# A pair of projection groups interleaved at the start, and the products with values in F32R parts

## What is computed

```python
xn = rmsnorm(h, norm_w[l], NORM_EPS)
proj = xn @ w_in[l]
o_ret = retention(rq, rk, rv).astype(h.dtype)        # (q k^T * decay) v, per head
o_ret = rmsnorm(o_ret, None, NORM_EPS).reshape(b, s, RET_WIDTH) * jax.nn.silu(rz)
o_diff = diff_attention(dq, dk, dv, lam)             # (softmax1 - lam * softmax2) v, per head
o_diff = rmsnorm(o_diff, subln_w[l], SUBLN_EPS) * (1.0 - lam_init) * jax.nn.silu(dz)
mixed = sigmoid(g_ret) * (o_ret @ w_ret_up) + sigmoid(g_diff) * (o_diff @ w_diff_up)
out = rmsnorm(h + mixed @ w_out, final_norm_w, NORM_EPS)
```

## Time and profile before

| | us |
|---|---|
| median of 3 runs (1103.31 to 1104.45) | 1103.32 |
| the profiled execution | 1103.43 |
| its span, from the first to the last instruction | 1101.6 |
| TensorE busy | 1088.8 |
| VectorE busy | 652.3 |
| ScalarE busy | 511.4 |

### The profile page before, as it was taken

How to read it: one execution, slowest core, us unless ns; L and a number is a source line. 1 busy time by engine, 2 the same in 40 slices (tenths; PEclk the granted TensorE clock), 3 DMA queues, 4 the chain that set the end, 5 groups by cost and what they waited for, 6 DMA issues and landing times.

```text
span 1101.6 us, 12909 instructions
## 1 busy us (share of the span) xinstructions
PE 1088.8 (99%) x4822; PEld 903.9 (82%) x4822; DVE 652.3 (59%) x785; ACT 511.4 (46%) x652; POOL 47.1 (4%) x64
## 2 busy tenths in 40 slices
PE   8999999999999999999999999999999999999997
PEld 6888888888888888888888888888888888888885
DVE  6665456475455554566656766576656665676554
ACT  6544444434445443334544464445444554444443
POOL 0100000000000000000010001000100010000111
PEclk9999999999999999999999999999999999999999
DMA  9876666667666655667566766766677666666862
GB/s 337 268 243 197 192 189 201 197 203 207 185 171 197 212 199 194 192 181 224 182 197 208 208 192 196 218 201 202 188 212 214 196 210 191 209 212 208 310 221 102
DMA packets 141030, 227.69 MB, mean 207 GB/s; under 512 B 14372, under 2 KB 40232, under 8 KB 140200
## 3 DMA queue, kind: packets, MB, share of 16 engines
q1 hardware_dynamic: 140408, 223.72, 66.1%
q10 hardware_dynamic: 560, 3.15, 0.7%
HBM read 210.58 MB, written 2.10 MB: 193 GB/s over the span
## 4 chain that ended last, share of the span: by engine, by line
PE 98%; DMA 1%; issue 1%; DVE 0%; SPq 0%; ACT 0%; ACTq 0%; POOLq 0%; POOL 0%; DVEq 0%
PE bank L1029 32%; PE bank L1031 31%; PE bank L1030 31%; PE bank L1036 1%; PE bank L1038 1%; PE bank L1037 1%; PE bank L1105 1%; DMA raw<-w_in_dram 1%; PE bank L1109 0%; PE bank L1060 0%; PE bank L1061 0%; DVE w_lo L706 0%; ACT w_hi L508 0%; ACT mixed L693 0%; DVE gate L958 0%
## 5 line engine op out<-in xcount | busy, mean ns | idle before, releaser
L706 DVE TENSOR_TENSOR w_lo<-raw,w_hi 128x1024 fp32r<-128x1024 f32 x383 | 474.2, 1243 | 421.3 <-ACT w_hi L508 420.3
L508 ACT ACTIVATE w_hi<-raw 128x1024 fp32r<-128x1024 f32 x383 | 405.7, 1060 | 549.6 <-PE bank L1031 518.1
L1029 PE MATMUL bank<-w_hi,xt_hi 128*128 128x512 f32 x1280 | 502.0, 392 | 2.8 <-DVE w_lo L706 2.8
L1031 PE MATMUL bank<-w_hi,xt_lo 128*128 128x512 f32 x1280 | 498.8, 390 | 0.0
L1030 PE MATMUL bank<-w_lo,xt_hi 128*128 128x512 f32 x1280 | 498.8, 390 | 0.0
L1029 PEld LDWEIGHTS bank<-w_hi,xt_hi 128*128 128x128 f32 x1280 | 240.6, 188 | 53.2 <-issue 3.5
L1031 PEld LDWEIGHTS bank<-w_hi,xt_lo 128*128 128x128 f32 x1280 | 240.7, 188 | 50.5
L1030 PEld LDWEIGHTS bank<-w_lo,xt_hi 128*128 128x128 f32 x1280 | 240.8, 188 | 49.5
L1029 PE MATMUL bank<-w_hi,ot_hi 128*128 128x512 f32 x256 | 99.6, 389 | 0.0
L1030 PE MATMUL bank<-w_lo,ot_hi 128*128 128x512 f32 x256 | 99.6, 389 | 0.0
L1031 PE MATMUL bank<-w_hi,ot_lo 128*128 128x512 f32 x256 | 99.6, 389 | 0.0
(11 more groups left out here) (99 smaller groups left out, 360.1 us busy)
## 6 DMA issues: line engine op xcount, KB each, us to landing
raw<-w_in_dram SPq DMA_DIRECT2D x287, 512.0 KB, 4.2
raw<-w_ret_up_dram SPq DMA_DIRECT2D x32, 512.0 KB, 4.2
raw<-w_diff_up_dram SPq DMA_DIRECT2D x32, 512.0 KB, 4.3
raw<-w_out_dram SPq DMA_DIRECT2D x32, 512.0 KB, 4.5
rot<-squares_t SPq DMA_DIRECT2D x96, 64.0 KB, 2.4
normed<-squares_t SPq DMA_DIRECT2D x48, 64.0 KB, 2.2
gate<-x_dram SPq DMA_DIRECT2D x2, 1024.0 KB, 9.0
kT<-squares_t SPq DMA_DIRECT2D x32, 64.0 KB, 2.2
```

What stands on the lines that cost most here:

```text
L508: act.activation(w_hi[:, s, :, :], raw[:, s, :, :], ACT.Copy).then_inc(hi_ready, 1)
L706: dve.tensor_tensor(w_lo[:, s, :, :], raw[:, s, :, :], w_hi[:, s, :, :].bitcast(F32), ALU.subtract) \
L1029: pe.matmul(bank[bk][:, :], hi, w_hi[:, s, kk, :], start=k == 0, stop=False)
L1031: return pe.matmul(bank[bk][:, :], lo, w_hi[:, s, kk, :], start=False, stop=k == KT - 1)
```

## The change

The first sixteen units, of the groups RQ and RK, are taken in a new order: first k-tiles 0 to 7 in pairs (RQ unit 0, RK unit 0, RQ unit 1, ...), then the rest of RQ, then the rest of RK. A pair of x tiles is thus needed at positions 0, 2, 4, 6 and 8 to 11. The second position is loaded and split in halves, as the first already was. The loads of x pairs, of the rows of x, of the rope tables and of decay move in SP's order; `square_x` moves from s = 6, 7 to 9, 10, and in the first iteration the rotation of Q from s = 10, 11 to 12, 13. `decay_sb` now lies in `gate`, where the rows of x were, and SP waits for their squares ahead of its load.

The products with values become three F32R passes each. ScalarE writes `v_hi` and the rounded part of the score maps (`read_keys_hi`, into the last k-tiles of `ot_hi`), VectorE the rests (`read_v_lo`, `read_keys_lo`), and the banks of the values are freed by VectorE's part. In attention the map is formed in `probs`, with one more step in its chain of waits, and VectorE's turning of it reads and writes contiguous runs.

```diff
 FIRST = UNITS - AHEAD
+ROTATE_Q = (12, 10)
...
+def pair_order():
+
+    for u in range(UNITS // 2):
+        for g in range(2):
+            yield g, u
+    for g in range(2):
+        for u in range(UNITS // 2, UNITS):
+            yield g, u
+
+
+PAIR = tuple(pair_order())
+X_PAIR_AT = {PAIR.index((0, j)): j for j in range(UNITS)}
+
+
+def unit_at(n):
+
+    return PAIR[n] if n < 2 * UNITS else (n // UNITS, n % UNITS)
 
 
...
-        decay_sb = sb("decay_sb", [P, HEADS, TOKENS])
...
-        v_sb = sb("v_sb", [P, BLOCKS, 2 * COLS])
+        v_hi = sb("v_hi", [P, BLOCKS, 2 * COLS], F32R)
+        v_lo = sb("v_lo", [P, BLOCKS, 2 * COLS], F32R)
...
+        decay_sb = gate[:, :, :].rearrange("p b n -> p (b n)")[:, 0:HEADS * TOKENS].rearrange("p (h t) -> p h t", h=HEADS)
...
-            return v_sb[:, a, COLS:COLS + 3 * P]
+            return probs[:, a * 6 * P:a * 6 * P + 3 * P]
...
-                s = u % RING
+                s = n % RING
...
+                elif n == 1:
+                    sp.dma_start(raw[:, s, 0, :], w[:, 0, col:col + COLS]).then_inc(half_landed[1], 16)
                     sp.dma_start(raw[:, s, 1:KU, :], w[:, 1:KU, col:col + COLS]).then_inc(raw_landed[s], 16)
...
-                        if s in (10, 11):
-                            turn_qk(qT, s - 10, ret_turns(it, 0))
+                        if s in (ROTATE_Q[it], ROTATE_Q[it] + 1):
+                            turn_qk(qT, s - ROTATE_Q[it], ret_turns(it, 0))
...
-                    if n in (1, 2, 3):
-                        load_x_t(sp, n, 1)
-                    if n in (4, 5):
-                        load_x_t(sp, 2 * n - 4, 2)
+                    if n in (2, 4, 6):
+                        load_x_t(sp, n // 2, 1)
+                    if n in (7, 9):
+                        load_x_t(sp, n - 3, 2)
...
-                    if n in (7, 8):
-                        b = n - 7
+                    if n in (10, 11):
+                        b = n - 10
                         sp.dma_start(gate[:, b, :], x[b * P:(b + 1) * P, :]).then_inc(x_landed, 16)
-                    if n == 9:
+                    if n == 12:
...
-                    if n == 14:
-                        sp.dma_start(decay_sb[:], decay).then_inc(decay_landed, 16)
+                    if n == 18:
+                        sp.wait_ge(x_squared, BLOCKS)
+                        sp.dma_start(decay_sb, decay).then_inc(decay_landed, 16)
...
-                    act.activation(v_sb[:, b, half * COLS:(half + 1) * COLS], bank[banks + b][:, :], ACT.Copy,
+                    act.activation(v_hi[:, b, half * COLS:(half + 1) * COLS], bank[banks + b][:, :], ACT.Copy,
                                    scale=x_rstd[:, b:b + 1]) \
-                       .then_inc(drained[banks + b], 1)
+                       .then_inc(v_hi_ready, 1)
+
+            def read_keys_hi(a, src, dst):
+                act.activation(dst, src, ACT.Copy).then_inc(keys_hi_ready, 1)
 
...
+                    if n0 + (s + AHEAD) in X_PAIR_AT:
+                        xt_hi_pair(X_PAIR_AT[n0 + (s + AHEAD)])
                     split_hi(n0 + (s + AHEAD), (s + AHEAD) % UNITS)
-                    if it == 0 and s in (6, 7):
-                        square_x(s - 6)
+                    if it == 0 and s in (9, 10):
+                        square_x(s - 9)
...
+                    if s in (36, 37):
+                        for m in range(2):
+                            act.wait_ge(drained[6 + m], ret_uses(it, 1) + 1)
+                        read_keys_hi(s - 36, scores_t(s - 36), keys_hi(s - 36))
+                    if s in (46, 47):
+                        act.wait_ge(filled[6 + s - 46], ret_uses(it, 2) + 1)
+                        read_keys_hi(s - 46, scores_t(s - 44), keys_hi(s - 46))
                     if s == 40:
...
+                    if s == 31:
+                        for a in range(2):
+                            act.wait_ge(turned[a], TURN * (diff_turns(it, 2) + 1))
+                            read_keys_hi(a, attn_strips(a), key_rows(keys_hi(a)))
...
+                elif event:
+                    dve.wait_ge(squares_ready[1], event)
...
+            def read_v_lo(count, banks, half):
+
+                for b in range(BLOCKS):
+                    cols = slice(half * COLS, (half + 1) * COLS)
+                    dve.wait_ge(v_hi_ready, count + (b + 1))
+                    dve.scalar_tensor_tensor(out=v_lo[:, b, cols], in0=bank[banks + b][:, :], scalar=x_rstd[:, b:b + 1],
+                                             in1=v_hi[:, b, cols].bitcast(F32), op0=ALU.mult, op1=ALU.subtract) \
+                       .then_inc(drained[banks + b], 1)
+
+            def read_keys_lo(count, src, hi, dst):
+
+                dve.wait_ge(keys_hi_ready, count + 1)
+                dve.tensor_tensor(dst, src, hi.bitcast(F32), ALU.subtract).then_inc(keys_lo_ready, 1)
...
-                    if s == 10:
+                    if s == q0:
                         dve.wait_ge(rope_ready, BLOCKS)
-                    if s in (10, 11):
-                        group_done(n0 + 7)
-                        rotate(0, it * 4 + (s - 10), 0, ret_uses(it, 0), s - 10, ret_turns(it, 0))
+                    if s in (q0, q0 + 1):
+                        group_done(n0 + q0 - 1 if it == 0 else n0 + 7)
+                        rotate(0, it * 4 + (s - q0), 0, ret_uses(it, 0), s - q0, ret_turns(it, 0))
...
+                    if s in (37, 38):
+                        read_keys_lo(it * 4 + (s - 37), scores_t(s - 37), keys_hi(s - 37), keys_lo(s - 37))
+                    if s == 41:
+                        read_v_lo(it * 4, 0, 0)
+                    if s in (47, 48):
+                        read_keys_lo(it * 4 + (2 + s - 47), scores_t(s - 45), keys_hi(s - 47), keys_lo(s - 47))
+                    if s == 49:
+                        read_v_lo(it * 4 + 2, 2, 1)
...
-                        turn_squares(a, diff_turns(it, 2), attn_of(a), 3 * SQUARE, False, True)
+                        turn_squares(a, diff_turns(it, 2), attn_of(a), 3 * SQUARE, False, False)
                     if s == 29:
                         gate_z(it * 2 + 4 * RET_ITS, 0, 0)
+                    if s == 32:
+                        for a in range(2):
+                            read_keys_lo(it * 2 + (4 * RET_ITS + a), attn_strips(a), key_rows(keys_hi(a)), key_rows(keys_lo(a)))
+                    if s == 33:
+                        read_v_lo(it * 2 + 4 * RET_ITS, 2, 0)
...
-                    if n < UNITS:
-                        pe.wait_ge(xt_lo_ready, KU * n + kk + 1)
+                    if n in X_PAIR_AT:
+                        pe.wait_ge(xt_lo_ready, KU * u + kk + 1)
                     if kk == 0 or u == 0:
                         pe.wait_ge(units_split, 2 * n + (2 * RING + (1 if u == 0 and kk == 0 else 2)))
                     for b in range(BLOCKS):
-                        mm = three_passes(u, kk, banks + b, b, left_hi, left_lo)
+                        mm = three_passes(n % RING, u, kk, banks + b, b, left_hi, left_lo)
...
-            def weights_by_v(dst, v_col, q0k0, q1k0, q1k1):
-
-                v0, v1 = v_sb[:, 0, v_col:v_col + V], v_sb[:, 1, v_col:v_col + V]
-                pe.matmul(dst[:, 0:V], q0k0, v0, start=True, stop=True)
-                pe.matmul(dst[:, V:2 * V], q1k0, v0, start=True, stop=False)
-                return pe.matmul(dst[:, V:2 * V], q1k1, v1, start=False, stop=True)
+            def keys_by_v(dst, a, x, b, v_col, start, stop):
+
+                hi, lo = keys_hi(a)[:, x * P:(x + 1) * P], keys_lo(a)[:, x * P:(x + 1) * P]
+                cols = slice(v_col, v_col + V)
+                pe.matmul(dst, hi, v_hi[:, b, cols], start=start, stop=False)
+                pe.matmul(dst, hi, v_lo[:, b, cols], start=False, stop=False)
+                return pe.matmul(dst, lo, v_hi[:, b, cols], start=False, stop=stop)
+
+            def weights_by_v(dst, a, v_col, q0k0, q1k0, q1k1):
+
+                keys_by_v(dst[:, 0:V], a, q0k0, 0, v_col, True, True)
+                keys_by_v(dst[:, V:2 * V], a, q1k0, 0, v_col, True, False)
+                return keys_by_v(dst[:, V:2 * V], a, q1k1, 1, v_col, False, True)
 
 
...
-                            st = scores_t(m)
-                            weights_by_v(bank[6 + m % 2], m * V, st[:, 0:P], st[:, P:2 * P], st[:, 2 * P:3 * P]) \
+                            pe.wait_ge(keys_lo_ready, it * 4 + (m + 1))
+                            weights_by_v(bank[6 + m % 2], m % 2, m * V, 0, 1, 2) \
...
-                            pe.wait_ge(turned[a], TURN * (diff_turns(it, 2) + 1))
+                            pe.wait_ge(keys_lo_ready, it * 2 + (4 * RET_ITS + a + 1))
                             pe.wait_ge(drained[6 + a], diff_uses_high(it, 3))
-                            weights_by_v(bank[6 + a], a * V, attn_keys(a, 2), attn_keys(a, 0), attn_keys(a, 1)) \
+                            weights_by_v(bank[6 + a], a, a * V, 2, 0, 1) \
```

(50 more changed lines are left out.)

38 lines of the change are left out of this document (23 added, 15 removed).

## The result

The changed kernel takes 1097.21 us in the median of four runs (1096.80 to 1097.25), the kernel before 1103.88 in four runs beside them (1103.31 to 1106.09). The ratio is 0.9945, with an interval of 0.9932 to 0.9957: faster by 0.55%. The forecast was 1096.3 with a range of 1094.3 to 1099.8. The profiled execution of after took 1097.22 us with a span of 1095.3, against 1103.43 and 1101.6 before: 6.2 us less.

What follows compares the result with a forecast made beforehand. The prediction took TensorE, busy 99% of the span, as the bound. From 1103.43 us it took 3.1 for the start and 3.9 for the products: 1096.4, or 1096.3 against the median, range 1094.3 to 1099.8.

Steps and rivals of the forecast that it cites:

- The sum: Whole kernel: 3.1 us from the start and 3.9 from the products, giving 1096.4, or 1096.3 against the median; chance 0.66.
- The start: First units: unit 2's first matmul moves from 16.52 to 13.46, 3.1 us gained, bounds 1.5 and 4.5.
- What the prediction gave the clock: Unit 1 at the start: about 1.6 us of its 4.41 went to TensorE's 1.2 GHz level after the idle stretch.
- rival (a): Start: idle times of 0.2 and 1.25 us still bring the 1.2 GHz level, 1.6 us comes back: 1098.0; chance 0.12.
- The products: Products with values, 8 groups: 18 F32R passes at 0.117 us replace 2.59 us; gain 0.49 per group, 3.9 in all.
- Rival (d): Products with values: at 256 columns the weight load is not hidden, a pass takes 0.188: 1106.6 us; chance 0.07.
- Rival (e): Products with values: the narrow F32R pass falls back to the fp32 pace, 0.43, 7.8 per group: 1142 us; chance 0.02.
- Attention's cover: Attention: VectorE's value rests end at 559.4, products start at 560.95; covered by 1.5 us, priced at nothing.
- Rival (c): Attention's products wait for VectorE's rests, some 3 us beyond the cover over four iterations: 1099.4; chance 0.05.
- The rotation's cover: Q's rotation ahead of unit 16: block 1's product ends at 48.9, unit 16 is due at 51.5; covered by 2.6 us.
- rival (b): The start gains nothing, because transfers decide or unit 16 waits for Q's rotation: 1099.5; chance 0.08.
- SP's wait ahead of decay: SP's queue: waits for squares of x, done about 39 us; unit 19 behind it not asked for before about 43; costs nothing.

Runs made afterwards that it cites:

- narrow: The changed kernel with each pass of the products with values cut into two of 128 columns, 36 per group instead of 18: 1112.41 us in one run.
- late_rests: The changed kernel with attention's value rests one unit later in VectorE's order (s = 34 instead of 33): 1102.59 us, ratio 0.9998 against the kernel before.
- f32r_only: The kernel before with the new F32R products and decay's new place and load, but the old order at the start: 1099.93 us, ratio 0.9971.
- pair_only: The kernel before with the new order, loads, halves and steps, but the old fp32 products with values: 1100.44 us, ratio 0.9978.

## Why the prediction was right, point by point

**The sum.** It forecast 3.1 + 3.9 = 7.0 us and got 6.2 in the profiled execution. Both terms were right in their mechanism and a little too large.

**The start**, unit 2 from 16.52 to 13.46: it came at 13.80, a gain of 2.7. The term that was off is the landing of unit 2's weights, 11.18 instead of 10.8; the 2.63 us from landing to matmul held (2.62). Placing landings by megabytes asked for gave the right place in the mean: the landing itself moves between executions, from 10.34 in `narrow` to 11.50 in `late_rests`, and the mean of the five starts, 13.44, is the forecast's. That it is so close is partly luck, with a spread of 1.15 us over five executions. Unit 1 followed unit 0 without the gap of 0.2 that was forecast: its first half was rounded at 7.53, so the weights landed near 7.5 (forecast 7.7). This helped nothing, as unit 2 then had to be waited for 1.95 us instead of 1.25.

**What the prediction gave the clock.** It counted 1.6 us of the start's gain as the end of the half clock, and rival (a) as its return. The size is about right: its rows give 4.41 - 2.72 = 1.69 us, and unit 1 in before against `f32r_only` gives 1.56. In after's profile the clock stayed at 1.00, so (a) did not happen. But the step took it for granted, from one profile, that before always pays these 1.6 us. Its runs show two levels, near 1102.0 and 1103.6. Against the first the change gains 4.7 us (1.1 at the start, as unit 2 stands at 14.86 in `f32r_only` and at 13.80 in after, and the rest at the products), against the second 6.4. The forecast of after's time doesn't depend on this, as the prediction set out from an execution of the slower level and took the 1.6 us off. But all four runs of before beside the result (1103.31 to 1106.09) lay on the slower level, where only about half of the 58 later ones did: that the ratio shows all of the gain is luck.

**The products.** 0.117 per pass was taken from between 0.113 and 0.120, and 0.120 was measured: the 0.0134 us left over per pass are paid once per pass, at 256 columns as at 512. The gain is 0.43 us per group by the chain, 3.4 in all, or 3.7 between the landmarks; the forecast had 3.9. Halving the wide pass had been given half of the weight, and has none.

**Rival (d), the weight load in the open.** Wrong, as the earlier trace rows said: loads of 0.19 us start 0.12 apart. The rule of the Trainium skill (TensorE: Matmul & The Clock Gate, Part 3, The mechanism), that a load overlaps only matmuls of other row groups, does not hold here: full-height passes follow at 0.120 with 0.107 of array time in them. What is true of the rival is a floor of 0.11, found with `narrow`; it doubles the price of a pass of 128 columns. Rival (e), a narrow F32R pass at 0.43, was wrong too (0.120).

**Attention's cover.** The timeline of after, one iteration:

```profile
543.33 2.49 SPq L388 DMA_DIRECT2D zs<-squares_t  x4
...
546.62 1.18 ACT L572 ACTIVATE ot_hi<-zs 128x384 fp32r<-128x384 f32 x2
...
550.87 1.01 DVE L826 TENSOR_TENSOR ot_lo<-zs,ot_hi 128x384 fp32r<-128x384 f32 x2
...
553.40 1.40 DVE L819 SCALAR_TENSOR_TENSOR v_lo<-bank,x_rstd,v_hi 128x512 fp32r<-128x512 f32 x2
...
556.33 0.28 PE L1146 MATMUL bank<-v_hi,ot_hi 128*128 128x256 f32 x1
```

The rests of the values end at 554.80 and the products start at 556.33: 1.5 us, as forecast. Rival (c) did not happen, and `late_rests` shows that its mechanism is real one unit further on.

**The rotation's cover.** The timeline of after:

```profile
34.65 1.06 ACT L551 ACTIVATE w_hi<-raw 128x1024 fp32r<-128x1024 f32 x1 [2.80 <-DMA raw<-w_in_dram]
35.62 1.04 ACT L613 ACTIVATE gate<-gate 128x1024 f32<-128x1024 f32 x1
...
43.54 0.47 SPq L457 DMA_DIRECT2D gate<-decay_dram  x1
...
44.88 0.69 DVE L801 TENSOR_TENSOR rot<-bank,rope_sb 128x512 f32<-128x512 f32 x1 [0.65 <-POOL rope_sb L499]
```

The squares start at 35.62, not at 33.5. The split ahead of them waits 2.80 us for its weights, which SP asks for at 25.52, behind both megabytes of x rows (20.97 and 24.00); the prediction let the squares start as soon as TensorE's progress allows this split, and had the late transfers only as a reserve. The rest of the chain is a little shorter than before (9.3 instead of 10.2), so that the rotation starts 1.2 us late, at 44.88, and its last read of the banks ends at about 50.0. Unit 16 is due at 13.80 + 38.1 = 51.9: a cover of 1.9 and not 2.6. The price of nothing was right, and so rival (b) was wrong in this half; in the other half (the start gains nothing) `pair_only` speaks against it, with 2.8 us. SP's wait ahead of decay cost nothing, as forecast: it is issued at 43.54, and TensorE waits for no unit behind it.

## What to carry to other kernels

At a start that transfers set, ask which piece of work lands last for the engine that must not idle, and cut that one: halving unit 1 was worth nothing that the times show while unit 2 was whole, and halving both gave 1.7 us more than the change. A pass of TensorE costs its columns plus a fixed part (here 0.013 us), down to a floor (0.11 us for a pass that brings its own load), and the duration of a load in the profile, 0.19 us, is not that floor: read the distance between two starts. Price a step whose last cover is about a microsecond by moving it a unit and seeing what shows; and before a gain is put down to the clock, look at several executions of the kernel before, since one profile shows only one of its levels.

## What the runs showed of the hardware that was not expected

The granted clock fell to half in the profiles of two executions of before, after TensorE had waited 2.76 and 2.54 us at the start, and in neither of the two profiles of the old order with the new products, after 2.33 and 2.21 us; after the 1.79 us of after it did not fall in the profile either. The times of before fall into two levels 1.7 us apart, and almost all of the faster ones have a mean clock of 0.998 or 0.999, all of the slower ones 0.996 or 0.997. What decides between the levels is open.

The pace of F32R passes with a weight load each is 0.227 us at 512 columns, 0.120 at 256 and 0.110 at 128, against an array time of 0.213, 0.107 and 0.053; the load's own duration is 0.19 us throughout.

Writing contiguous runs hardly made VectorE's turning of the score map cheaper: 860 ns for 128 x 384 in after, 872 before. Only the writes changed: in both kernels it reads every fourth element, other than the section on the change says.
